# Moving the input norm, the small loads and the constants at the start of a two-layer mixer and mixture-of-experts kernel

## What is computed

```python
def _layernorm(t, g, b):
    mu = jnp.mean(tf, -1, keepdims=True)
    var = jnp.mean(jnp.square(tf - mu), -1, keepdims=True)
    out = (tf - mu) * lax.rsqrt(var + LN_EPS) * g + b
    ...
h = _layernorm(x, ln_in_g, ln_in_b)
for layer in range(DEPTH):          # DEPTH = 2
    proj = jnp.einsum('bsd,de->bse', h, w_in[layer])
    ...                             # three attentions, gates, w_out
    h = _layernorm(DEEPNORM_ALPHA * h + y, ln_g[layer], ln_b[layer])
...                                 # second block, then 32 experts, top 4 of each token
```

## Time and profile before

| | us |
|---|---|
| median of 3 runs (lowest, highest) | 1880.21 (1879.91, 1883.44) |
| profiled execution, whole | 1882.82 |
| its span in the trace | 1881.0 |
| PE busy in the span | 1648.2 (88%) |
| DVE, ACT busy | 392.8, 300.3 |
| moved by DMA | 515 MB, mean 274 GB/s |

### The profile page before, as it was taken

How to read it: one execution, slowest core, us unless ns; L and a number is a source line. 1 busy time by engine, 2 the same in 40 slices (tenths; PEclk the granted TensorE clock), 3 DMA queues, 4 the chain that set the end, 5 groups by cost and what they waited for, 6 DMA issues and landing times.

```text
span 1881.0 us, 19486 instructions
## 1 busy us (share of the span) xinstructions
PE 1648.2 (88%) x7938; PEld 969.1 (52%) x7938; DVE 392.8 (21%) x881; ACT 300.3 (16%) x587; POOL 2.8 (0%) x9
## 2 busy tenths in 40 slices
PE   3998799988799576869799999999999999999996
PEld 3786577857687465758633343333333333333342
DVE  2103411071101623721211111111111111111111
ACT  2013311151302401220200110110101001010010
POOL 0000000000000000000000000000000000000000
PEclk7998899999899777879799999999999999999998
DMA  7347534482233112203499999999999999999994
GB/s 251 133 125 227 187 106 155 143 313 74 79 114 134 45 45 90 90 31 149 148 402 427 428 429 429 428 429 428 428 429 429 429 428 429 428 428 429 429 428 202
DMA packets 86184, 515.04 MB, mean 274 GB/s; under 512 B 7000, under 2 KB 10776, under 8 KB 61560
## 3 DMA queue, kind: packets, MB, share of 16 engines
q1 hardware_dynamic: 82328, 513.43, 67.9%
q10 hardware_dynamic: 3632, 0.54, 0.2%
q0 software_dynamic: 176, 0.39, 0.1%
HBM read 511.20 MB, written 3.15 MB: 273 GB/s over the span
## 4 chain that ended last, share of the span: by engine, by line
PE 68%; DMA 17%; DVE 7%; ACT 4%; issue 2%; ACTq 1%; DVEq 0%; SPq 0%
PE psum L439 25%; PE psum L930 18%; DMA ring<-in_w_gu 15%; PE psum L999 8%; PE psum L903 3%; PE psum L448 3%; PE psum L479 2%; PE psum L913 2%; DMA ring<-in_w_ada 2%; PE psum L921 1%; DMA w_router<-in_w_router 1%; DVE sc L1405 1%; PE psum L496 1%; PE psum L815 1%; PE psum L480 1%
## 5 line engine op out<-in xcount | busy, mean ns | idle before, releaser
L930 PE MATMUL psum<-ring,hg 128*64 128x512 f32 x2048 | 458.6, 596 | 21.4 <-DMA ring<-in_w_gu 21.4
L439 PE MATMUL psum<-hT,ring 128*128 128x256 f32 x1504 | 342.4, 391 | 6.2 <-ACT hT L1190 6.2
L439 PEld LDWEIGHTS psum<-hT,ring 128*128 128x128 f32 x1504 | 296.0, 197 | 52.5 <-issue 9.9
L930 PEld LDWEIGHTS psum<-ring,hg 128*64 128x64 f32 x2048 | 139.2, 137 | 312.4 <-issue 267.7
L999 PE MATMUL psum<-w_down,hiddenT 128*64 128x512 f32 x1024 | 229.3, 600 | 28.2 <-ACT hiddenT L1365 25.2
L999 PEld LDWEIGHTS psum<-w_down,hiddenT 128*64 128x64 f32 x1024 | 74.9, 138 | 162.2 <-issue 162.2
L1767 DVE TENSOR_SCALAR gu<-psum 128x512 f32<-128x512 f32 x32 | 22.1, 692 | 529.2 <-PE psum L930 529.2
L1361 ACT ACTIVATE hidden<-gu 128x512 f32<-128x512 f32 x32 | 20.2, 630 | 316.2 <-DVE gu L1767 316.2
L439 PE MATMUL psum<-yT,ring 128*128 128x256 f32 x256 | 60.9, 403 | 9.3 <-DVE yT L1397 9.3
L903 PE MATMUL psum<-pick,h_tok 128*128 128x128 f32 x512 | 63.5, 284 | 2.9 <-DVE passes L1750 2.9
L903 PEld LDWEIGHTS psum<-pick,h_tok 128*128 128x128 f32 x512 | 60.5, 197 | 8.2 <-issue 8.2
(11 more groups left out here) (348 smaller groups left out, 1283.8 us busy)
## 6 DMA issues: line engine op xcount, KB each, us to landing
ring<-in_w_gu SPq DMA_DIRECT2D x128, 2048.0 KB, 22.5
w_down<-in_w_dn SPq DMA_DIRECT2D x64, 2048.0 KB, 20.7
ring<-in_w_in SPq DMA_DIRECT2D x24, 2048.0 KB, 8.0
ring<-in_w_ada SPq DMA_DIRECT2D x12, 2048.0 KB, 10.6
ring<-in_w_out SPq DMA_DIRECT2D x6, 2048.0 KB, 9.9
ring<-in_w_in SPq DMA_DIRECT2D x2, 2064.0 KB, 7.8
ring<-in_w_ssm_o SPq DMA_DIRECT2D x2, 2048.0 KB, 7.8
ring<-in_w_in SPq DMA_DIRECT2D x1, 2112.0 KB, 8.1
```

What stands on the lines that cost most here:

```text
L439: mm = pe.matmul(bank[0:m, c * T:(c + 1) * T], w[:, k, c0 + c * P:c0 + c * P + m], src[:, k, :], start=(k == 0), stop=(k == k_n - 1))
L930: mm = pe.matmul(psum[half * CAP:(half + 1) * CAP, 4 + part, :], hg[:, k, side, :], w[:, c0:c0 + 512], start=False, stop=(k == KC - 1), sk ...
```

## The change

The input norm is computed with tokens on partitions: DVE takes mean and variance along the row with `bn_stats` (two halves of 512 for each block of 128 tokens) and `bn_aggr`, ACT makes rstd from it, DVE normalises `x_in` in place, and PE transposes the normalised x. Gain and bias are applied as the banks are read into `hT`: chunks 0, 1, 4, 5 by ACT, 2, 3, 6, 7 by DVE. For this only the rows of `ln_in_g` and `ln_in_b` are needed early (ACT still issues them) and the identity, which gets a DMA of its own. The mean and variance matmuls of this norm are gone, and so are its `h_ready` counts (all later counts are 4 lower). The other 31 small loads are issued by SP behind the groups q0 and k0, then the rest of `k_all` and `k_first`, then the groups va0, ga0. PE's "vecs" and "bias" stand behind the k0 projections (`late_constants`), ACT's part in `condT` and `lam` behind its reads of q and k.

```diff
 # tensor: head of the program
-        pe.wait_ge(ev("const_in"), 32)
-        pe.wait_ge(ev("means_set"), 6)
-        pe.wait_ge(ev("x_in"), 16)
-        for c in range(0, KC, 2):
...
-        norm_sums("in.", [f"x{c}" for c in (0, 2, 4, 6)])
...
+        pe.wait_ge(ev("ident_in"), 16)
+        pe.wait_ge(ev("ln_in"), 32)
+        bank = take("ln_in")
+        mm = pe.transpose(bank[:, 0:2 * KC], vec_rows[0:2 * KC, 0, :], ident[0:2 * KC, 0:2 * KC])
+        full(mm, "ln_in")
+        x_banks = [take(f"x{c}") for c in range(0, KC, 2)]
+        for b in range(NB):
+            for c in range(KC):
+                if c % 4 == 0:
+                    pe.wait_ge(ev("x_norm"), 2 * b + c // 4 + 1)
+                at = (c % 2 * NB + b) * P
+                mm = pe.transpose(x_banks[c // 2][:, at:at + P], x_in[:, b, c * P:(c + 1) * P], ident[:, :])
+                if b == NB - 1 and c % 2:
+                    full(mm, f"x{c - 1}")
+        def late_constants():
+            pe.wait_ge(ev("const_in"), 32)
+            pe.wait_ge(ev("means_set"), 6)
+            pe.wait_ge(ev("rows_in"), 16 * (len(row_loads) - 2 + 2 * len(twice)))
...
 # in features
+                    if ready == 0 and c == 0 and k % 2 == 0:
+                        read_out(pe, f"x{k}")
 # behind the projections q and k
+            if l == 0:
+                late_constants()
 # sync
-        sp.dma_start(x_in[:, :, :], a["x"][0].rearrange("(b p) d -> p b d", p=P)).then_inc(ev("x_in"), 16)
-        for pack in (False, True):
-            sp.dma_start(const_tiles[pack][:, :], packs[pack][1][:, :]).then_inc(ev("const_in"), 16)
+        for b in range(NB):
+            sp.dma_start(x_in[:, b, :], a["x"][0, b * P:(b + 1) * P, :]).then_inc(ev(f"x_in{b}"), 16)
+        sp.dma_start(const_tiles[False][:, 0:P], packs[False][1][:, 0:P]).then_inc(ev("ident_in"), 16)
...
+            if g == 1:
+                load_small()
+                sp.dma_start(const_tiles[False][:, P:], packs[False][1][:, P:]).then_inc(ev("const_in"), 16)
+                sp.dma_start(const_tiles[True][:, :], packs[True][1][:, :]).then_inc(ev("const_in"), 16)
 # scalar
+        for tile, at, n, src in row_loads[:2]:
+            act.dma_start(vec_rows[at:at + n, tile, :], src).then_inc(ev("ln_in"), 16)
...
+        for b in range(NB):
+            act.wait_ge(ev("x_stats"), b + 1)
+            f(x_rstd[:, b:b + 1], x_mean[:, b, 1:2], ACT.Ln, bias=eps[:, 0:1])
+            f(x_rstd[:, b:b + 1], x_rstd[:, b:b + 1], ACT.Exp, ev("x_rstd"), scale=-0.5)
+        read_out(act, "ln_in")
+        for c in (0, 1, 4, 5):
+            x, at = product(act, f"x{c // 2 * 2}"), c % 2 * T
+            ins = act.activation(hT[:, c, :], x[:, at:at + T], ACT.Identity, bias=vec("ln_in_b", c),
+                                 scale=vec("ln_in_g", c))
...
 # vector
-        for c in range(0, KC, 2):
-            ch.free(dve.tensor_copy(xT[:, c:c + 2, :], two(product(dve, f"x{c}"))), f"x{c}")
+        for b in range(NB):
+            dve.wait_ge(ev(f"x_in{b}"), 16)
+            for j in range(2):
+                ch.after(dve.bn_stats(x_stats[:, b, j, :], x_in[:, b, 512 * j:512 * j + 512]))
+            ch.after(dve.bn_aggr(x_mean[:, b, :], x_stats[:, b, :, :]), ev("x_stats"))
+        for b in range(NB):
+            dve.wait_ge(ev("x_rstd"), b + 1)
+            for j in range(2):
+                r = slice(512 * j, 512 * j + 512)
+                ts(x_in[:, b, r], x_in[:, b, r], x_mean[:, b, 0:1], x_rstd[:, b:b + 1], ALU.subtract, ALU.mult,
+                   s=ev("x_norm"))
...
-        norm("in.", True, hT)
```

More of the change, by code:

```diff
@@ L220, in mixer_moe_kernel @@
     cumq = sb("cumq", [P, NB * HB], where=first)
+    x_stats = sb("x_stats", [P, NB, 2, 6], where=first)
+    x_mean = sb("x_mean", [P, NB, 2], where=first)
+    x_rstd = sb("x_rstd", [P, NB], where=first)
     first.close()
@@ L436, in features @@
                 for k in range(k_n):
-                    if ready is not None and c == 0 and k % 2 == 0:
-                        pe.wait_ge(ev("h_ready"), 4 * ready + k // 2 + 1)
+                    if ready == 0 and c == 0 and k % 2 == 0:
+                        read_out(pe, f"x{k}")
+                    elif ready is not None and c == 0 and k % 2 == 0:
+                        pe.wait_ge(ev("h_ready"), 4 * ready + k // 2 - 3)
                     mm = pe.matmul(bank[0:m, c * T:(c + 1) * T], w[:, k, c0 + c * P:c0 + c * P + m],
@@ L569, in _ @@
-        full(mm, "bias")
+        pe.wait_ge(ev("ident_in"), 16)
[12 more added lines that the diff above has]
+                    full(mm, f"x{c - 1}")
@@ new lines, in late_constants @@
+        def late_constants():
+            pe.wait_ge(ev("const_in"), 32)
+            pe.wait_ge(ev("means_set"), 6)
+            pe.wait_ge(ev("rows_in"), 16 * (len(row_loads) - 2 + 2 * len(twice)))
+            bank = take("vecs")
+            for t in range(2):
+                mm = pe.transpose(bank[:, t * P:t * P + vec_tiles[t]], vec_rows[0:vec_tiles[t], t, :],
+                                  ident[0:vec_tiles[t], 0:vec_tiles[t]])
+            full(mm, "vecs")
+            bank = take("bias")
+            pe.wait_ge(ev("bcast_in"), 16 * N_BCAST)
+            mm = pe.matmul(bank[0:AH, :], rel_bias[:, :], K["hot"][0:32, :], start=True, stop=True)
+            full(mm, "bias")
@@ L860, in _ @@
         norm_sums("f.", None)
-        pe.wait_ge(ev("h_ready"), 4 * (DEPTH + 3))
+        pe.wait_ge(ev("h_ready"), 4 * (DEPTH + 2))
         bank = take("router")
@@ L1052, in _, with load_small @@
     def _(sp):
-        sp.dma_start(x_in[:, :, :], a["x"][0].rearrange("(b p) d -> p b d", p=P)).then_inc(ev("x_in"), 16)
-        for pack in (False, True):
-            sp.dma_start(const_tiles[pack][:, :], packs[pack][1][:, :]).then_inc(ev("const_in"), 16)
+        for b in range(NB):
+            sp.dma_start(x_in[:, b, :], a["x"][0, b * P:(b + 1) * P, :]).then_inc(ev(f"x_in{b}"), 16)
+        sp.dma_start(const_tiles[False][:, 0:P], packs[False][1][:, 0:P]).then_inc(ev("ident_in"), 16)
+        def load_small():
+            for tile, at, n, src in row_loads[2:]:
+                sp.dma_start(vec_rows[at:at + n, tile, :], src).then_inc(ev("rows_in"), 16)
+            for at, src in twice:
+                for half in range(2):
+                    sp.dma_start(vec_rows[at:at + 1, 1, half * HEAD:(half + 1) * HEAD], src)\
+                        .then_inc(ev("rows_in"), 16)
+            alike = [(lam_in[:, i, :], a[n].rearrange("l d -> (l d)")) for i, n in
+                     enumerate(("lambda_q1", "lambda_k1", "lambda_q2", "lambda_k2"))]
+            alike += [(b_forget[:, :], a["b_forget"].rearrange("l h -> (l h)")), (dt_bias[:, :], a["dt_bias_2"][0]),
+                      (a_log[:, :], a["a_log_2"][0]), (b_router[:, :], a["b_router_2"][0])]
+            for dst, src in alike:
+                sp.dma_start(dst, src.partition_broadcast(P)).then_inc(ev("bcast_in"), 16)
+            for half in range(2):
+                src = a["d_skip_2"][0].rearrange("(c two) -> two c", two=2)[half]
+                with nc.allow_non_contiguous_dma(reason="16 numbers"):
+                    sp.dma_start(d_skip[half * HEAD:(half + 1) * HEAD, :], src.partition_broadcast(HEAD))\
+                        .then_inc(ev("bcast_in"), 16)
+            sp.dma_start(rel_bias[:, :], a["rel_bias_2"]).then_inc(ev("bcast_in"), 16)
+            sp.dma_start(w_router[:, :, :], a["w_router_2"][0].rearrange("(k p) n -> p k n", p=P))\
+                .then_inc(ev("bcast_in"), 16)
         for g, (name, src) in enumerate(groups):
@@ L1068, in _ @@
                 sp.wait_ge(ev("bias_out"), 16)
-                sp.wait_ge(ev("h_ready"), 4 * (DEPTH + 1))
+                sp.wait_ge(ev("h_ready"), 4 * DEPTH)
                 for qb in range(NB):
@@ L1090, in load @@
                 if first:
-                    sp.wait_ge(ev("h_ready"), 4 * (DEPTH + 3))
+                    sp.wait_ge(ev("h_ready"), 4 * (DEPTH + 2))
                 else:
@@ L1115, in _ @@
     def _(pool):
-        pool.wait_ge(ev("h_ready"), 4 * (DEPTH + 3))
+        pool.wait_ge(ev("h_ready"), 4 * (DEPTH + 2))
         pool.dma_start(b_dn[:, :], a["b_dn_2"][0]).then_inc(ev("b_dn_in"), 16)
@@ L1184, in norm @@
             rstd(tag + "var", stat[:, :], e, ev("rstd"), cols=slice(0, T))
-            if tag == "in.":
-                read_out(act, "vecs")
             for j in range(4):
@@ L1194, in _ @@
         centrings = [0]
+        exp_table()
         act.wait_ge(ev("means_set"), 6)
[L1196 to L1200, removed]
+        for b in range(NB):
[7 more added lines that the diff above has]
+                                 scale=vec("ln_in_g", c))
+            if c % 2:
+                ch.free(ins, f"x{c - 1}")
+            else:
+                ch.after(ins)
         for l in range(DEPTH):
@@ L1205, in _ @@
                 read(f"{L}{'qk'[j // 2]}{j % 2}", qk_raw[:, 2 * j:2 * j + 2, :])
+            if l == 0:
+                read_out(act, "vecs")
```

(20 more changed lines are left out.)

## The result

The changed kernel takes 1850.53 us (median of 4, 1848.88 to 1852.32) against 1881.83 (median of 4, 1879.91 to 1884.57): a ratio of 0.9833, interval 0.9814 to 0.9852. The profiled execution took 1852.01 us, its span 1850.2, 30.8 us less than before.

What follows compares the result with a forecast made beforehand. PE's chain before SP's issue at 938 us, ahead of the saturated expert stream, sets the end. va0 at 12.3 + 30.2 + 1.1 = 43.6 instead of 73.57 saves 30.0: 1880.2 - 30.0 = 1850.2 us, range 1846 to 1863.

Steps and rivals of the forecast that it cites:

- First projection at 12.3: PE's first projection would start at 12.3 us instead of 43.35, set about equally by q0's weights and bank x0.
- q and k as before, 30.2 us: From first projection to the late constants, PE's q and k would keep their 30.2 us, cold-start price of 2.4 included.
- rival 4: Clock rises early, during the transposes before q and k: 2.4 us more gain, 1847.8; counted inside the forecast, no separate chance.
- Late constants 1.1: PE's "vecs" and "bias" products behind q and k would take 1.1 us, about half their earlier time, at high clock.
- Cost of the small loads 12 us, 3.6 us of slack: Ahead of va0, SP's 31 small loads would occupy the queue about 12 us (17 to 29), leaving 3.6 us spare.
- Rival 1: Small loads, standing before the tables and va0, become the wait: 1855 to 1876 us; chance 0.16.
- no DMA as the releaser of va0: Sign in the changed trace: va0 starts at 43 to 44 us without a DMA ending PE's wait.
- Nothing given back later: After va0, the ada wait (30.6 us) and experts shift with PE, so the whole 30.0 us gain reaches the end.
- The expert stream follows: In the saturated expert part, landmarks come 30 us earlier and two experts still take 58.7 us.
- Rival 2: Each small load on SP's queue pays full latency in turn, 84 us for 31, giving 1918 us; chance 0.03.
- the estimate from the Trainium skill: Small loads at about 2.0 us fixed each plus bytes over 436 GB/s: 62 us in series, kernel some 15 slower.

Runs made afterwards that it cites:

- the part-change on the kernel before: Kernel before the change, with only the bias product, condT and lam moved behind the q and k projections: 1874.26 us, ratio 0.9957.
- the one with the early write: Changed kernel with d_skip and w_router loads behind ga0, plus the bias_scratch write issued by ACT behind lam instead of SP behind ada0: 1841.10 us.
- the repair of the queue: Changed kernel with the two d_skip loads issued behind ga0 and awaited where they are used: 1848.38 us, ratio 0.9816.

## Why the prediction was right, point by point

- *First projection at 12.3.* 12.53. Statistics: 1.42 us for two passes, 0.71 each (0.69 taken), aggregation 0.21; the first half of x had landed at 4.71 (4.7). Normalisation 2.29 / 4 = 0.57 (0.49 taken), transposes 3.67 (3.54), gain and bias on ACT 2.35 / 4 = 0.59 (0.5). PE and the q0 weights were ready together, as said: in the other traces of the same start the last wait is 0.2 to 0.3 us for q0.
- *q and k as before, 30.2 us.* Here the step that failed was keeping the price of the cold start. From 12.53 to the late constants at 40.49 it took 28.0: the windows show a granted clock of 1.00 all the way, and the 128 products of ga0, at 1.00 too, take 27.6. This is the variant priced as rival 4, and it gave 2.3 us.
- *Late constants 1.1.* From 40.49 to 41.78, 1.3.
- *Cost of the small loads 12 us, 3.6 us of slack.* This term was mis-sized. k0 landed at 17.8 (17.5), the last small load at 33.6 and not 29, so 15.8 us instead of 12, and va0 at 44.2 and not 40. The bounds 8.9 and 40.6 held it, and the choice near the low end was wrong for a reason that can be named: from the trace before, only the packets' share beside weights could be read, 185 GB/s at 23 to 30 us; alone in a queue the 4-byte pieces leave the engines with 14 GB/s. SP's issues were faster than thought (it was through with the 31 at 21.2, in spite of 5.6 us of standing at the first), so the rate of issue played no part.
- *Rival 1* therefore came true in kind, with a small price: 2.45 us of waiting and 1.6 for va at a lower clock, for which the prediction had no term. The sign it had named, no DMA as the releaser of va0, did not hold. The two errors, 2.3 less for the cold start and 2.5 more for the wait, nearly cancelled: va0 at 44.2 instead of 43.6. That va0 came out so close is partly luck, and with va's low clock the gain at ga0 was only 27.6 of the 30.0 forecast.
- *Nothing given back later.* Nearly: the two waits for ada grew from 4.7 us (the earlier trace rows is their chain) to 7.1, but the chain through them only from 30.6 to 31.5. And something was given on top, without which the end would have gained some 28 us: 0.6 us between the ada wait and out0, where the mean granted clock was 0.94 instead of 0.87, and more later: between the landmarks at 757.73 and 827.01 before (729.23 and 796.24 after) the time fell by 2.3 us. The windows, before and after:

```profile
757.73:827.01 69.28, 50.48 (x233) 39.47 (x233) 41.96 (x102) 21.98 (x54) 0.00 (x0) 0.80 0.17 61
```

```profile
729.23:796.24 67.01, 47.97 (x232) 37.82 (x233) 41.94 (x102) 21.97 (x54) 0.00 (x0) 0.84 0.18 63
```

  DVE and ACT did the same work in the same time; PE's was 2.5 us shorter at a higher mean clock. That has nothing to do with the change's intent, and the part-change on the kernel before (69.3 us there as well) lacks it. Why the kernels with the new queues or the new norm take 67.0 us there (67.4 the one with the early write) is open. So the mechanism was right but the hit on the total, 1850.5 against 1850.2, is luck to the extent of about 3 us.
- *The expert stream follows.* Two experts take 58.7 us as in the earlier trace rows, and the chain's last waits stand 30.6 us earlier.
- *Rival 2* (latencies in turn) is out: 8 broadcasts issued 0.47 us apart landed some 4 us after their issue each. Nor was the estimate from the Trainium skill, "DMA: Bandwidth & Descriptors", section on the anatomy of one DMA, met with its fixed cost in series; that section gives the figure for DMAs issued from GpSimd, and these were issued by SP, a difference that the prediction passed over.

## What to carry to other kernels

At the start of a kernel an engine that issues DMAs can't compute, and everything that a first product doesn't read should be behind what it reads, both in the issuing engine's program and in the queue. A small load is priced by how many and how short its pieces are, not by its bytes: look for 4-byte runs, load them as rows and spread them on chip. Compare the time at which a transfer's source is ready with the time of its issue: a write that stood 45 us behind its source, ahead of weights, was worth more (6.3 us) than the repair of the queue (4.6), and it had stood there before the change too.

## What the runs showed of the hardware

- 1024 pieces of 4 bytes in one queue held it for 9.5 us with the DMA engines busy for 12%; a second 1024 cost 10.4 more. 128 rows of 64 bytes for the same data cost nothing that shows, and 1024 pieces of 128 bytes landed in 3.4 us. Beside full weight traffic in another queue they had looked like a loss of rate only.
- `bn_stats` on 128x512 fp32 takes 0.71 us, `bn_aggr` of two such 0.21: mean and variance of 128 tokens of width 1024 in 1.63 us, so 3.3 for all 256. With features on partitions the kernel before spent 3.6 and 5.9 us on PE, 2.5 on DVE and 2.2 on ACT for the 256 (the 5.9 were 3.7 in the kernel with the new queues and the old norm).
- A PE idle for 2.4 us at 42 us found its clock at 1.2 GHz afterwards (0.50 granted up to 47 us), which cost 1.6 us in va; in the kernels in which va0 did not wait it stayed at 2.4 (1.00 from 41.32 to 55.30).
- SP stood 5.6 us at the issue of a load of 8 KB, from 3.32 us on, with 5184 KB issued ahead of it; in the kernel before, with 4870 KB ahead, it stood 3.5 us at the issue of k0.
